# Causal attention with rotary scores on both row halves in turn, score turns ahead of the next scores, and the next head's projections inside a head's last steps

## The reference, cut to what matters

```python
q = (rmsnorm(q_lat, q_norm_g) @ w_qb).reshape(B, S, N_HEADS, QK_NOPE + QK_ROPE)
q_nope, q_pe = jnp.split(q, [QK_NOPE], axis=-1)
kv = (rmsnorm(kv_lat, kv_norm_g) @ w_kvb).reshape(B, S, N_HEADS, QK_NOPE + V_HEAD)
k_nope, v = jnp.split(kv, [QK_NOPE], axis=-1)
q_pe = apply_rope(q_pe, cos[:, :, None, :], sin[:, :, None, :])
k_pe = apply_rope(k_pe, cos, sin)
...
s = jnp.einsum('bqhd,bkhd->bhqk', qi.astype(jnp.float32), kf) * scale
mask = kpos[None, :] <= qpos[:, None]
s = jnp.where(mask[None, None], s, -jnp.inf)
p = jax.nn.softmax(s, axis=-1).astype(v.dtype)
...
return (o * jax.nn.silu(gate)) @ w_out
```

## Time and profile before

| | us |
|---|---|
| median of 3 runs | 4370.37 |
| lowest and highest run | 4364.6, 4372.84 |
| the profiled execution's own time | 4368.24 |
| its span in the profile | 4366.4 |
| TensorE busy in the span | 4249.0 |
| the stage of the eight heads, from 1620.50 to 2007.16 | 386.66 |

### The profile page before, as it was taken

The page is one execution under the profiler, slowest core; times in us unless marked ns, Lnnn a source line. Parts: engine busy times, 40 slices in busy tenths (PEclk is TensorE's granted clock), DMA queues, the critical chain, the costliest instruction groups (busy, mean ns, idle before and its releaser), DMA issues.

```text
span 4366.4 us, 45768 instructions
## 1 busy us (share of the span) xinstructions
PE 4249.0 (97%) x19364; PEld 2209.1 (51%) x19364; DVE 1685.9 (39%) x2686; ACT 851.8 (20%) x1639; POOL 783.7 (18%) x519
## 2 busy tenths in 40 slices
PE   8999999999999999999999999999999999999999
PEld 4458444444444446665444444564489544444444
DVE  4635373333324323332499540343533322222311
ACT  2114130000002113221133211453134200000000
POOL 5213034323200110000164200000000022221310
PEclk9999999999999999999999999999999999999999
DMA  5420001111110220000111111101010121111121
GB/s 196 165 86 1 29 23 45 48 39 48 39 48 29 78 82 13 13 11 29 39 39 39 39 53 53 49 18 54 34 38 4 49 77 49 39 48 39 69 79 45
DMA packets 52571, 215.53 MB, mean 49 GB/s; under 512 B 5856, under 2 KB 7392, under 8 KB 50448
## 3 DMA queue, kind: packets, MB, share of 16 engines
q1 hardware_dynamic: 47808, 168.58, 11.0%
q0 software_dynamic: 4560, 44.02, 2.6%
HBM read 193.71 MB, written 18.87 MB: 49 GB/s over the span
## 4 chain that ended last, share of the span: by engine, by line
PE 92%; DVE 4%; POOL 1%; ACT 1%; issue 1%; DMA 1%; SPq 0%; DVEq 0%; POOLq 0%; ACTq 0%
PE bank L474 32%; PE bank L183 30%; PE bank L2760 4%; PE bank L2578 4%; PE bank L1700 2%; PE bank L1753 2%; PE bank L2771 2%; PE bank L1736 1%; PE bank L1739 1%; PE bank L2467 1%; PE bank L2451 1%; PE bank L2482 1%; PE bank L1716 1%; PE bank L2749 1%; PE bank L2701 1%
## 5 line engine op out<-in xcount | busy, mean ns | idle before, releaser
L183 PE MATMUL bank<-H,ring 128*128 128x512 f32 x1920 | 835.5, 596 | 10.7 <-ACT H L371 4.7
L183 PEld LDWEIGHTS bank<-H,ring 128*128 128x128 f32 x1920 | 365.5, 191 | 470.4 <-issue 455.6
L183 PE MATMUL bank<-ABC,ring 128*128 128x512 f32 x1200 | 520.8, 594 | 3.0 <-POOL ABC L1654 2.6
L183 PEld LDWEIGHTS bank<-ABC,ring 128*128 128x128 f32 x1200 | 227.1, 190 | 287.2 <-issue 280.0
L474 PE MATMUL bank<-H,ring 128*128 128x512 f32 x736 | 323.4, 592 | 0.8 <-ACT ABC L1799 0.8
L2065 DVE SCALAR_TENSOR_TENSOR bank<-ABC,params,bank 128x1024 f32<-128x1024 f32 x184 | 237.3, 1290 | 8.3 <-DVE ABC L2042 0.5
L474 PEld LDWEIGHTS bank<-H,ring 128*128 128x128 f32 x736 | 139.8, 190 | 177.1 <-issue 177.1
L474 PE MATMUL bank<-H,X 128*128 128x512 f32 x400 | 179.9, 592 | 0.3 <-POOL H L825 0.3
L474 PE MATMUL bank<-X 128*128 128x512 f32 x400 | 179.8, 592 | 0.0
L2578 PE MATMUL bank<-H 64*64 64x64 f32 x5088 | 168.3, 219 | 9.3 <-DVE H L3196 6.0
L2578 PEld LDWEIGHTS bank<-H 64*64 64x64 f32 x5088 | 159.2, 135 | 14.2 <-DVE H L3196 5.3
(11 more groups left out here) (543 smaller groups left out, 5931.8 us busy)
## 6 DMA issues: line engine op xcount, KB each, us to landing
ABC<-in_ada SPq DMA_DIRECT2D x48, 512.0 KB, 5.7
ring<-in_gu SPq DMA_DIRECT2D x44, 512.0 KB, 4.4
ring<-in_up SPq DMA_DIRECT2D x32, 512.0 KB, 4.0
ring<-in_down SPq DMA_DIRECT2D x32, 512.0 KB, 4.3
ring<-in_conv_in SPq DMA_DIRECT2D x24, 512.0 KB, 4.2
ring<-in_ffn SPq DMA_DIRECT2D x16, 704.0 KB, 4.7
ring<-in_proj SPq DMA_DIRECT2D x16, 512.0 KB, 6.6
ring<-in_mix SPq DMA_DIRECT2D x16, 512.0 KB, 4.5
```

The costliest lines, as they stand in the source:

```text
L183: mm = nc.tensor.matmul(bank[:, 2 * (m % 2) + h, :], ring[:, s % RING, k * P:(k + 1) * P], rhs(k)[:, h * HALF:(h + 1) * HALF], start=(k == ...
```

## The change

**Rotary scores.** `q_pe` keeps the rotary queries of the even head of a pair in its low 64 rows and of the odd head in the high 64. A new tile `q_swap` holds them the other way round: after `q_pe` is made, GpSimd issues two transfers of 64 rows. The rotary keys stand in both row halves of `k_pe`, and are no longer zeroed. So each head has its rotary queries and keys in either half, and a rotary product contracts over 64 rows, in either. `scores(hd, n)` makes the scores of two steps, n and n + 1, at once: first all plain products, then rotary pieces of up to 256 columns, low half and high half in turn. At step 0 the low half has bank 0 and the short block, the high half bank 1; at the other steps the low half has bank 0, the high half bank 1 and the short block.

**Order.** Turn g stands ahead of scores g + 2 and g + 3. The values are projected in two halves, before and after the first scores. The next head's queries are projected in steps 6 and 7, the rotary rows of a next pair before output 7, the keys after it. ScalarE and VectorE are written in the matching order.

```diff
-            k_pes = [k_pe, Hf[:, 6 * SEQ:7 * SEQ]]
+            q_swap = Hf[:, 6 * SEQ:7 * SEQ]
+            row_halves = [slice(0, 64), slice(64, 128)]
...
-            pool.wait_ge(*taken("mla_in"))
-            pool.memset(k_pes[1][0:64], 0.0).then_inc(*rope_pool.did("zero_low"))
-            pool.wait_ge(*rope_dve.all())
-            pool.wait_ge(*rope_pool.after(0, "zero_low"))
-            nc.gpsimd.tensor_copy(k_pes[1][64:128], k_pe[64:128]).then_inc(*rope_pool.did("copied"))
-            pool.wait_ge(*rope_pool.after(0, "copied"))
-            pool.memset(k_pe[64:128], 0.0).then_inc(*rope_pool.did("zero_high"))
-            pool.wait_ge(*mla_pe.all(lead=1))
+            for hd in range(0, HEADS, 2):
+                pool.wait_ge(*mla_dve.after(0, f"qpe_{hd}"))
+                for e in range(2):
+                    pool.dma_start(q_swap[row_halves[1 - e]], q_pe[row_halves[e]]).then_inc(q_swapped, 16)
+            pool.wait_ge(*mla_pe.all())
...
-                if e == 0:
-                    rows("pe", 4, 7, 3, 0)
-                rows("q", 0, 0, 3, 0)
-                if e == 0:
-                    pe.wait_ge(*now(mla_act, "pe"))
-                    for h in range(2):
-                        mm = nc.tensor.matmul(bank[:, 4 + h, :], rot, q_raw[:, h * HALF:(h + 1) * HALF], start=True, stop=True)
-                    mm.then_inc(*mla_pe.did("rot_0"))
-                rows("k", 2, 3, 2, 3)
-                for c in range(NT):
+            tile_of = lambda hd, k: ring[:, (t0 + hd) % RING, k * P:(k + 1) * P]
+
...
+            def key_rows(hd, h):
+                if hd and h == 0:
+                    pe.wait_ge(*mla_dve.after(0, f"min7_{hd - 1}"))
+                mm = rows(hd, 2, 3, 2, 3, h)
+                if h:
+                    mm.then_inc(*mla_pe.did(f"k_{hd}"))
+
+            def value_rows(hd, h):
+                if hd:
+                    pe.wait_ge(*(mla_dve.after(0, f"gated7_{hd - 1}") if h else mla_act.after(0, f"on7_{hd - 1}")))
+                for c in range(4 * h, 4 * h + 4):
                     for k in range(2):
-                        mm = nc.tensor.matmul(bank[:, 6 + c // 4, (c % 4) * P:(c % 4 + 1) * P],
-                                              A[:, 3 + k, c * P:(c + 1) * P], w(5 + k), start=(k == 0), stop=(k == 1))
-                mm.then_inc(*mla_pe.did(f"v_{e}"))
-
...
-                            pe.wait_ge(*rope_pool.all())
-                        if n >= 2:
-                            pe.wait_ge(*now(mla_dve, f"min{n - 2}"))
-                        width = (b + 1) * P
-                        now_at = slice(b * P, (b + 1) * P)
-                        for a in range(0, width, HALF):
-                            z = min(width, a + HALF)
-                            out_ = score_bank(n)[:, a:z]
-                            mm = nc.tensor.matmul(out_, q_n[:, now_at], k_n[:, a:z], start=True, stop=False)
-                            if n == 0 and a == 0:
-                                mm.then_inc(products_done, 2)
-                            mm = nc.tensor.matmul(out_, q_pe[:, now_at], k_pes[e][:, a:z], start=False, stop=True)
-                        mm.then_inc(*mla_pe.did(f"s{n}_{e}"))
-                    if 0 <= g < NT:
-                        pe.wait_ge(*now(mla_act, f"exp{g}"))
-                        if g >= 2:
-                            pe.wait_ge(*now(mla_dve, f"pt{g - 2}"))
-                        for k in range(LENGTHS[g] + 1):
-                            mm = nc.tensor.transpose(turn_bank2(g)[:, k * P:(k + 1) * P], p_exp(g)[:, k * P:(k + 1) * P], ident[:, :])
-                        mm.then_inc(*mla_pe.did(f"turn{g}_{e}"))
-                    if 0 <= g - 1 < NT:
-                        n = g - 1
...
+            def rotary_scores(hd, n, low, a, z):
+                own_half = q_pe if low == (hd % 2 == 0) else q_swap
+                side = row_halves[0 if low else 1]
+                return nc.tensor.matmul(score_bank(n)[:, a:z], own_half[side, LENGTHS[n] * P:(LENGTHS[n] + 1) * P], k_pe[side, a:z],
+                                        start=False, stop=True, skip_group_check=True)
+
+            def scores(hd, n):
+
+                if n == 0:
+                    pe.wait_ge(*mla_act.after(0, f"q_{hd}"))
+                    pe.wait_ge(*mla_act.after(0, f"k_{hd}"))
+                parts = []
+                for m in (n, n + 1):
+                    if m >= 2:
+                        pe.wait_ge(*mla_dve.after(0, f"min{m - 2}_{hd}"))
+                    b = LENGTHS[m]
+                    width = (b + 1) * P
+                    for a in range(0, width, HALF):
+                        z = min(width, a + HALF)
+                        nc.tensor.matmul(score_bank(m)[:, a:z], q_n[:, b * P:(b + 1) * P], k_n[:, a:z], start=True, stop=False,
+                                         skip_group_check=True)
+                        parts.append([(m, c, min(z, c + HALF // 2)) for c in range(a, z, HALF // 2)])
+                if n == 0:
+                    pe.wait_ge(*mla_dve.after(0, f"qpe_{hd - hd % 2}"))
+                    pe.wait_ge(q_swapped, 32 * (hd // 2 + 1))
+                low, high, short = parts
+                (low if n == 0 else high).extend(short)
+                pieces = [(on_low, *side[i]) for i in range(max(len(low), len(high)))
+                          for on_low, side in ((True, low), (False, high)) if i < len(side)]
+                last_of = {m: at for at, (on_low, m, a, z) in enumerate(pieces)}
+                for at, (on_low, m, a, z) in enumerate(pieces):
+                    mm = rotary_scores(hd, m, on_low, a, z)
+                    if at == last_of[m]:
+                        mm.then_inc(*mla_pe.did(f"s{m}_{hd}"))
+
...
+                    mm = nc.tensor.transpose(turn_bank2(g)[:, k * P:(k + 1) * P], p_exp(g)[:, k * P:(k + 1) * P], ident[:, :])
+                    if g == 0 and k == 0:
+                        mm.then_inc(products_done, 2)
+                mm.then_inc(*mla_pe.did(f"turn{g}_{hd}"))
...
+            rotary_rows(0)
+            query_rows(0, 0)
+            query_rows(0, 1)
+            rotary_turned(0)
+            key_rows(0, 0)
+            key_rows(0, 1)
+            for hd in range(HEADS):
+                after = hd + 1 if hd + 1 < HEADS else None
+                value_rows(hd, 0)
+                scores(hd, 0)
+                value_rows(hd, 1)
+                for g in range(NT):
+                    weights_turned(hd, g)
+                    if g % 2 == 0 and g + 2 < NT:
+                        scores(hd, g + 2)
+                    if after and g >= 6:
+                        query_rows(after, g - 6)
+                    if g >= 1:
+                        head_out(hd, g - 1)
+                    if g >= 2:
+                        out_turned(hd, g - 2)
+                if new_pair(after):
+                    rotary_rows(after)
+                head_out(hd, 7)
+                out_turned(hd, 6)
+                if after:
+                    key_rows(after, 0)
+                    if new_pair(after):
+                        rotary_turned(after)
+                    key_rows(after, 1)
+                out_turned(hd, 7)
+            pe.wait_ge(*mla_dve.all())
             pe.wait_ge(*taken("mla_heads"))
...
+            for hd in range(HEADS):
+                after = hd + 1 if hd + 1 < HEADS else None
+                values_kept(hd, 0)
+                if hd == 1:
                     gate_silu(2)
-                for what, b, dst, scale in (("pe", 4, q_raw, MLA_SCALE), ("q", 0, q_n, MLA_SCALE), ("k", 2, k_n, 1.0),
-                                            ("v", 6, v_tok.rearrange("p s n -> p (s n)"), 1.0)):
-                    if what == "pe" and e:
-                        continue
-                    act.wait_ge(*now(mla_pe, what))
-                    nc.scalar.activation(dst, two_banks(b), ACT.Identity, scale=scale).then_inc(*mla_act.did(f"{what}_{e}"))
-                for g in range(-2, NT + 2):
-                    if g + 2 < NT:
-                        n = g + 2
-                        scored = p_exp(n)[:, 0:(LENGTHS[n] + 1) * P]
-                        act.wait_ge(*now(mla_dve, f"min{n}"))
-                        nc.scalar.activation(scored, scored, ACT.Exp, scale=-1.0, bias=row_least[:, n % 4:n % 4 + 1],
-                                             accum_out=row_sum[:, n % 4:n % 4 + 1]).then_inc(*mla_act.did(f"exp{n}_{e}"))
-                    if 0 <= g - 1 < NT:
-                        n = g - 1
-                        act.wait_ge(*now(mla_pe, f"o{n}"))
-                        act.wait_ge(*now(mla_dve, f"recip{n}"))
-                        nc.scalar.activation(o_tok[:, n % 2, :], bank[:, 6, 0:P], ACT.Identity,
-                                             scale=row_recip[:, n % 4:n % 4 + 1]).then_inc(*mla_act.did(f"on{n}_{e}"))
+                weights(hd, 0)
+                values_kept(hd, 1)
+                weights(hd, 1)
+                for g in range(NT):
```

(29 more changed lines are left out.)

216 lines of the change are left out of this document (120 added, 96 removed).

## The result

| | before | after |
|---|---|---|
| median of the runs shown with the result, us | 4369.89 (4 runs) | 4343.51 (4 runs, 4337.79 to 4349.6) |
| ratio to before, 95% interval | | 0.9941 [0.9929, 0.9953] |
| the same kernel once more, later | 4369.65 (9 runs) | 4346.45 (5 runs), 0.9949 [0.9936, 0.9963] |
| the profiled execution: its time, its span | 4368.24, 4366.4 | 4340.04, 4338.2 |
| the stage of the eight heads | 386.66 | 361.84 |

The forecast was 4344 with 4335 to 4360, and the stage at 361.0. The new kernel is faster by 0.5 to 0.6%, 23 to 26 us.

A forecast was written before the change was run, and what follows sets the result against it. TensorE was taken to bound the stage: 353.7 - 25.7 columns + 11.2 groups + 17 gaps + 3.9 transfer + 0.9 gates = 361.0 against 386.7, 25.7 less, giving 4344 us for the kernel, range 4335 to 4360.

The forecast's parts named there:

- Rotary columns, -25.7: Rotary scores of eight heads: fewer product columns in sequence on TensorE save 25.7 us, a middle between 27.4 and 24.0.
- free halves: Rotary groups: each row half runs on by itself, 2,560 columns in sequence a head, saving 27.4 us over eight heads.
- lockstep: Rotary groups: a short piece holds the other half up, two groups a head last 768 columns, saving 24.0 us.
- rival 4: Rotary groups: short pieces of two groups hold up the other half, saving 24.0 for 25.7; time 4346; chance 40%.
- Rival 2: Rotary pieces do not run side by side; all 25.7 us lost, 4370, no change; chance 4%.
- Groups, +11.2 at 0.35 each: Rotary scores: each of 32 groups on the row halves costs 0.35 us extra, 11.2 in all (6.4 to 16).
- Gaps after, 17: TensorE's waits at turns and outputs in the new order: 17 us with restarts, where 33 stood before.
- Rival 1: The gaps stay: waits leaving scores 2 come back at turns and outputs, 33 for 17; 4360; chance 5%.
- Transfer, 3.9: Rotary products of pairs 1 to 3 wait 1.3 us each for the swapped queries, 3.9 in all; pair 0 nothing.
- Gates, 0.9: Head 1: two gate activations on ScalarE stand ahead of exp 0 and delay it by 0.9 us, once.
- D: Landing time of the rotary query copy (two 256 KB transfers), taken as 4.0 us; TensorE waits D - 2.7.
- 353.7: The stage of the eight heads without its known gaps: 386.7 - 33 = 353.7 us.

The follow-up runs named there:

- halves_apart: All low-half rotary pieces listed ahead of all high-half ones, instead of in turn, against the changed kernel: 4351.21 us, stage 362.10 against 361.84.
- one_half: All rotary pieces on the low row half, order and transfers kept, against the changed kernel: 4375.14 us, stage 394.19, 32.4 more.
- order_only: The changed kernel's new order, but rotary scores over 128 rows with zeroed keys as before the change: 4360.52 us, stage 372.32.
- halves_only: The kernel before, in its old order, with each block's rotary scores put on both row halves: 4366.47 us, stage 383.32, 3.3 less than before.
- values_first: All sixteen value products ahead of the first scores, against the changed kernel: 4368.14 us, stage 383.77, 21.9 more.
- swap_chained: Second transfer of each pair issued only when the first has landed, against the changed kernel: 4358.12 us, stage 373.62, 11.8 more.

## Why the prediction was right, point by point

**What bounds the kernel.** Right. The stage is TensorE's, and its 24.8 us came in part from columns (19.0 less busy) and in part from gaps.

**Rotary columns, -25.7.** The step was a middle between free halves (27.4) and lockstep (24.0). The halves are free. The timeline of TensorE in head 0 of the changed kernel at the group of scores 2 and 3 (blocks 6 and 1), with the plain scores before it and the turns and the output behind it:

```profile
1643.59 2.10 PE L1771 MATMUL bank<-ABC 128*128 128x512 f32 x6
1645.62 0.48 PE L1755 MATMUL bank<-ABC 64*128 64x256 f32 x1
...
1646.90 0.33 PE L1792 MATMUL bank<-ident,H 128*128 128x128 f32 x1
1647.07 1.95 PE L1801 MATMUL bank<-H 128*128 128x128 f32 x16
1649.12 0.98 PE L1792 MATMUL bank<-ident,H 128*128 128x128 f32 x7
```

The group lasts 1646.90 - 1645.62 = 1.28, and that of blocks 4 and 3 takes 1.29 in the chain. The group of blocks 5 and 2, which has 640 columns in either case, takes 1.28 too (1784.14 in the chain). In lockstep the first two would be a record of 256 columns, 0.21, longer than the third. And halves_apart rules out program order by 20 us. The term is 27.4, and rival 4 (40%) was a false alarm of 1.7 us. Rival 2 fell with it, at the 0.85 a group that one_half shows.

**Groups, +11.2 at 0.35 each.** 0.39 from order_only, 0.36 from halves_only: 12.6. In a group's own row only 1.29 - 1.07 = 0.22 is seen, as in the earlier trace rows. The rest lies before and behind it: from the start of the plain scores to the start of the group are 2.03 in the rows above and 1.94 between the same places of order_only, and the single transpose behind the group takes 0.17 to the next start, for 0.11 there. The bounds of 0.2 to 0.5 were right to reach above what the row shows.

**Gaps after, 17.** The list was right, and its sum a little low. Measured: turn 0 idle 5.0, of which 1.4 is head 1's, so (5.0 - 1.4) / 7 = 0.51 in the others, against 0.5 forecast. Turn 2 waits 0.10 in each head: in the rows above the output is over at 1647.07 + 1.95 = 1649.02 and the turn starts at 1649.12. Outputs 2 and 4 in the chain of head 3:

```profile
1786.39 1.80 PE bank L1801 x14
...
1793.27 0.11 issue
1793.38 1.58 PE bank L1801 x12
```

Output 2 waits 0.22, output 4 0.11. Behind each wait the row is longer than its records alone: 1.07 for eight transposes of 0.11, 0.98 for seven, 1.80 for 14 output records of 0.112 and 1.58 for 12, so a restart is 0.19 to 0.24, nearer 0.22 than the 0.26 of the forecast. With it turn 0 costs 0.7 for 0.8, turn 2 0.3 for 0.2, output 2 0.45 for 0.4, output 4 0.35 for 0.3. The tail's output 7 and the last head have 2.2 + 0.5 + 0.4 in seven waits and with restarts 4.6, against 3.4. All idle time without transfer and gates is 16.1 - 4.5 - 0.9 = 10.7, in 39 places, with 39 restarts of 0.22 19.3 for 17. Rival 1 had 33.

**Transfer, 3.9.** 4.5 idle in three waits. Their restarts are nearly hidden in the cost of the group, whose eight records take 1.15 behind a wait and 1.09 without: 4.7. Pair 0 has none, as forecast. The landing was 3.6 for the second transfer of a pair and with GpSimd's issue of 0.50, which I had not counted apart from it, D is 4.4 for 4.0. The estimate from the Trainium skill ("DMA: Bandwidth & Descriptors", section "Anatomy of one DMA — SWDGE (gpsimd) path") was 3.1 for the pair and 0.4 of wait. The trace has 2.73 to 2.79 for one alone, near the page's 2.6, and 3.6 for the second of two, with a wait of 1.5. The page's sum holds for a lone transfer and was too low for the overlap.

**Gates, 0.9.** 1.4 of wait in head 1 against 0.51 elsewhere: 0.9. The timeline of ScalarE there, in the place of the earlier trace rows:

```profile
1678.15 0.60 ACT L1900 ACTIVATE H<-bank 128x512 f32<-128x512 f32 x1 [0.87 <-PE bank L1748]
1678.76 1.28 ACT L1884 ACT_TABLE_LOAD   x1
1680.06 2.00 ACT L1884 ACTIVATE ABC<-ABC 128x1024 f32<-128x1024 f32 x2
```

**The sum.** 353.7 - 27.4 + 12.6 + 19.3 + 4.7 + 0.9 = 363.8, against 361.8 measured and 361.0 forecast. The terms' errors were -1.7 (columns), +1.4 (groups), +2.3 (gaps) and +0.8 (transfer), 2.8 in all, and the 2.0 by which their sum is too long lies in the 353.7: that term was what the known gaps left over in the kernel before, and something of it did not come along into the new order; what, is not shown. So the middle of the forecast came out within 0.8 us of the stage partly by luck, since errors of one to two us cancel in it; the mechanism, the places of the waits and the order of their sizes did not need that luck. Nor could the total tell rival 4: only the length of a group and halves_apart did. Two slips of the prediction are small: 4342.5 and 2.1 make 4344.6, not 4344; and its own range, worked out with all its ends, would run from 4333.6 to 4362, since the upper end left out the 4.8 of groups at 0.5 and the lower one was rounded in by 1.4.

## What to carry to other kernels

- Products on 64 rows pay only when both row halves work at once, and each group costs about 0.4 us however short it is. So gather the short ones: in 64 groups the rotary products took TensorE about as long as on full rows (its busy time rose by 3.5 us, and the stage's 3.3 us came from waits), in 32 groups, with the order that allows them, they took 14.9 us less and the stage 10.5.
- Take the list of waits after a change and ask of each what could lie under it; two value products more under turn 0, a transfer that starts one step earlier and two activations moved gave another 7.6 us, a third of what the change gave.
- Count an exposed wait of 2.5 us on TensorE as more than its length. In values_first each was followed by a stretch at half clock that cost another 1.4 to 1.5 us (11.6 / 8).

## What the runs showed of the hardware

- TensorE starts a product ahead of products listed before it when its row half is free (halves_apart: starts 10 ns apart, stage 362.10, where starts in listed order were expected to give 382). What signals the end of a product may still go by the list: the signal for the minimum at the group shown is on the last high piece of scores 2, the one of 128 columns, over at 1646.54 + 0.38 = 1646.92. The minimum began at 1647.18, just after 1646.74 + 0.38 = 1647.12, when the low piece listed before it was over. In the changed kernel the high piece of the same group is over at 1646.54, the low one at 1646.37 + 0.38 = 1646.75, and the minimum begins at 1646.80. Ends of products are modelled in this profile, and this is read from these groups and was not tried apart.
- TensorE's granted clock falls from its full 2.4 to 1.2 GHz in the midst of a busy stage, at the end of single waits or soon behind them: in all eight heads of values_first (waits of 2.48 us; 11.6 us in all), after the three transfer waits of 3.5 us in swap_chained (5.8 us), and after those of 1.5 us in one_half (8.5 us more busy time). It did not fall after the 1.5 us waits of the changed kernel. The edit between these two kernels is only whether the rotary products fill one row half or both; whether that is the cause was not tried apart.
- Work behind the touched stage took 2357 us (the changed kernel) to 2365 us (order_only) with the same instructions, and all work outside the stage 3976 to 3986 us. With a single profile, differences under 10 us are better read in a stage than in the span.
